# Expert stage of a two-layer encoder: two wide phases, gate and up in chunks of their own, another order of the slots

## What is computed

```python
logits = jnp.dot(xt, router_w, preferred_element_type=jnp.float32)
top_val, top_idx = lax.top_k(logits, TOP_K)
top_w = jax.nn.softmax(top_val, axis=-1)
...
def swiglu(h, w_gate, w_up, w_down):
    return (jax.nn.silu(h @ w_gate) * (h @ w_up)) @ w_down
```

## Time and profile before

| what | us |
|---|---|
| median of 3 runs | 1406.99 (1406.58 to 1407.42) |
| span of the profiled execution | 1403.7 |
| TensorE busy, share of the span | 1304.4, 93% |
| VectorE busy | 415.5 |
| ScalarE busy | 290.6 |
| bytes moved by transfers | 481.98 MB, mean 343 GB/s |

### The profile page before, as it was taken

One profiled execution on the slowest core, in us unless ns is written; L12 is line 12 of the kernel. 1 busy time (PEld: TensorE's weight loads), 2 busy tenths in 40 slices (PEclk: granted clock), 3 DMA queues, 4 the chain that ended last, 5 costly groups with the idle time before them and its releaser, 6 DMA issues.

```text
span 1403.7 us, 24351 instructions
## 1 busy us (share of the span) xinstructions
PE 1304.4 (93%) x10626; PEld 690.9 (49%) x10627; DVE 415.5 (30%) x789; ACT 290.6 (21%) x524; POOL 32.5 (2%) x82
## 2 busy tenths in 40 slices
PE   5999999999999999999999999999589998988986
PEld 5767888888778576243333334333134332324221
DVE  4876844444468664200200000300001200001001
ACT  3346533434333552010000001000001000001000
POOL 1002000000000020000000000000000000000000
PEclk9999999999999999999999999999899999999999
DMA  9988665444575799999989999999999999999996
GB/s 347 332 342 317 198 229 190 180 179 179 223 256 210 325 367 365 400 404 409 407 352 404 365 398 409 408 408 408 409 395 408 409 409 409 409 397 401 408 402 266
DMA packets 146005, 481.98 MB, mean 343 GB/s; under 512 B 9032, under 2 KB 11152, under 8 KB 140784
## 3 DMA queue, kind: packets, MB, share of 16 engines
q1 hardware_dynamic: 141952, 475.06, 87.2%
q10 hardware_dynamic: 2720, 2.93, 0.8%
q0 software_dynamic: 1232, 2.50, 0.6%
HBM read 477.32 MB, written 1.05 MB: 341 GB/s over the span
## 4 chain that ended last, share of the span: by engine, by line
PE 61%; SPq 23%; DMA 7%; DVE 4%; ACT 2%; issue 2%; POOL 0%; DVEq 0%; ACTq 0%
PE ps L2472 19%; SPq L765 15%; PE ps L2524 9%; PE ps L2160 8%; PE ps L2162 8%; PE ps L2161 8%; SPq L779 7%; DMA raw<-in_moe_w_down_dram 4%; PE ps L2082 2%; PE ps L2539 1%; DMA weights<-in_ada_w_dram 1%; DVE weights_lo L1257 1%; PE ps L2241 1%; DMA weights<-in_w_in_dram 1%; PE ps L2214 1%
## 5 line engine op out<-in xcount | busy, mean ns | idle before, releaser
L2472 PE MATMUL ps<-raw,hX 128*32 128x512 f32 (+1 forms) x4416 | 474.2, 583 | 36.0 <-DMA raw<-in_moe_w_up_dram 19.0
L2472 PEld LDWEIGHTS ps<-raw,hX 128*32 128x32 f32 x4416 | 141.2, 110 | 338.9 <-issue 302.7
L2524 PE MATMUL ps<-raw,m_actT 128*32 128x512 f32 x1568 | 180.8, 611 | 18.3 <-DMA raw<-in_moe_w_down_dram 18.2
L2160 PE MATMUL ps<-weights_hi,hT_hi 128*128 128x512 f32 (+1 forms) x416 | 162.1, 390 | 2.7 <-DVE hT_lo L1360 1.5
L2162 PE MATMUL ps<-weights_hi,hT_lo 128*128 128x512 f32 (+1 forms) x416 | 158.9, 382 | 0.0
L2161 PE MATMUL ps<-weights_lo,hT_hi 128*128 128x512 f32 (+1 forms) x416 | 158.7, 381 | 0.0
L1648 DVE TENSOR_TENSOR m_actX<-m_sgX,ps 128x256 f32<-128x256 f32 (+1 forms) x20 | 7.8, 388 | 406.5 <-ACT m_sg L1108 279.9
L2524 PEld LDWEIGHTS ps<-raw,m_actT 128*32 128x32 f32 x1568 | 54.5, 112 | 136.3 <-issue 125.9
L1257 DVE TENSOR_TENSOR weights_lo<-weights,weights_hi 128x2048 fp32r<-128x2048 f32 (+1 forms) x52 | 113.1, 2202 | 2.4 <-ACT weights_hi L934 1.1
L934 ACT ACTIVATE weights_hi<-weights 128x2048 fp32r<-128x2048 f32 (+1 forms) x48 | 87.2, 1839 | 55.6 <-PE ps L2162 51.4
L1651 DVE TENSOR_TENSOR m_act<-m_sg,ps 128x512 f32<-128x512 f32 (+2 forms) x20 | 16.1, 805 | 265.9 <-ACT m_sg L1108 265.9
(11 more groups left out here) (277 smaller groups left out, 1051.0 us busy)
## 6 DMA issues: line engine op xcount, KB each, us to landing
raw<-in_moe_w_gate_dram SPq DMA_DIRECT2D x112, 1024.0 KB, 16.8
raw<-in_moe_w_up_dram SPq DMA_DIRECT2D x112, 1024.0 KB, 18.4
raw<-in_moe_w_down_dram SPq DMA_DIRECT2D x110, 1024.0 KB, 16.8
weights<-in_ada_w_dram SPq DMA_DIRECT2D x18, 2048.0 KB, 9.9
weights<-in_ffn_w_gate_dram SPq DMA_DIRECT2D x14, 1024.0 KB, 5.6
weights<-in_ffn_w_up_dram SPq DMA_DIRECT2D x14, 1024.0 KB, 8.2
weights<-in_ffn_w_down_dram SPq DMA_DIRECT2D x7, 2048.0 KB, 9.6
weights<-in_w_in_dram SPq DMA_DIRECT2D x6, 2048.0 KB, 12.7
```

The costliest lines, as they stand in the source:

```text
L2160: pe.matmul(dst, stat_hi, hi, start=start, stop=False, skip_group_check=True)
L2472: mm = pe.matmul(ps[32 * q:32 * q + 32, bank, 0:2 * w].rearrange("p (g n) -> p g n", g=2), hX[:, k, at32:at32 + 32], weights[:, kk, :, at: ...
L2524: mm = pe.matmul(ps[32 * quarter:32 * quarter + 32, bank, col:col + w], stationary[:, 32 * half:32 * half + 32], raw[buffer][:, D * j + w ...
```

## The change

- Two phases of 2048 and 1536 columns in place of four. A unit is now a whole bank of 512 columns (`COL`, 384 in the second phase) of gate alone; ACT writes its silu to SBUF, then the same bank takes the up sums, and DVE multiplies. TensorE counts up `part` after each unit, so that ACT and DVE go unit by unit; `turned` and `copied` count units too.
- A gate chunk or an up chunk has two k rows of 2048 or 1536 columns: loads of 128 x 2048 (8 KB a row) or 128 x 1536 (6 KB a row). In the second phase a chunk is 1.5 MiB.
- Down chunks take the hidden rows in pairs: partition p holds rows 2p and 2p + 1 of 256, which lie side by side in memory (8 KB); in the second phase a pair and a single row (4 KB). The transposes read the product's columns with a step of two to match.
- Order of a step on TensorE: four gate chunks, two down chunks of the step before, four up chunks, two more down chunks, transposes.
- Slots are now A, X, ABX, X, AX, AB, X, A, in groups (0), (1), (2, 3), (4), (5, 6), (7); banks for gathers and added rows follow.
- The tail is the last two down chunks, in two and three loads.
- Tiles move: some share places with tiles that are no longer needed then. On DVE, `shares`, `token_rows` and `row_numbers` come one phase earlier.

```diff
-NPH = 4
-WIDE = (1024, 1024, 1024, 512)
+NPH = 2
+WIDE = (2048, 1536)
+COL = (512, 384)
 HU = 256
-GU_CHUNKS = (4, 4, 4, 2)
-DOWN_CHUNKS = (2, 2, 2, 1)
+KINDS = ("gate", "up", "down")
+CHUNKS = 4
+
+
+DOWN_RUNS = (((0, 2), (2, 2)), ((0, 2), (2, 1)))
+J = [sum(r for _, r in runs) for runs in DOWN_RUNS]
 RAWS = 9
 EARLY = 2
...
 
-SLOT_RANK = (0, 1, 6, 3, 7, 2, 5, 4)
-SLOT_PASSES = ("A", "ABX", "X", "AX", "X", "AB", "X", "A")
-GROUPS = ((0,), (1, 2), (3, 4), (5, 6), (7,))
+SLOT_RANK = (0, 5, 1, 6, 3, 2, 7, 4)
+SLOT_PASSES = ("A", "X", "ABX", "X", "AX", "AB", "X", "A")
+GROUPS = ((0,), (1,), (2, 3), (4,), (5, 6), (7,))
 OVER_PASSES = "AB"
...
 
+def units_of(passes):
+
+
+    return [(c, b) for c in passes for b in range(len(UNIT_BANKS[c]))]
+
+
+def turn_order(passes):
+
+    return sorted(units_of(passes), key=lambda unit: unit[0] != "X")
+
+
 def chunk_order():
 
     order = []
     for s, n in STEPS:
-        order += [("gu", s, n, i) for i in range(GU_CHUNKS[n])]
-        for t, m in ended_by(s, n):
-            order += [("down", t, m, i) for i in range(DOWN_CHUNKS[m])]
+        for kind, down in (("gate", (0, 1)), ("up", (2, 3))):
+            order += [(kind, s, n, i) for i in range(CHUNKS)]
+            order += [("down", t, m, i) for t, m in step_before(s, n) for i in down]
+        if n == NPH - 1 and s >= LAST - 1:
+            order += [("down", s, n, i) for i in range(CHUNKS)]
     return order
 
...
             def load_chunk(z, sig, e, kind, n, i):
                 b = z.buffer(kind, n, i)
-                if kind == "gu":
-                    per = CH // (2 * WIDE[n])
+                if kind != "down":
                     dst = gu_view(raw[b], n)
-                    for g, view in enumerate((moe_gate_v, moe_up_v)):
-                        src = view[bass.ds(e, 1), :, per * i:per * i + per, 1024 * n:1024 * n + WIDE[n]]
-                        sp.dma_start(dst[:, :, g, :], src.rearrange("a p k n -> p (a k) n")).then_inc(
+                    view = moe_gate_v if kind == "gate" else moe_up_v
+                    for kk in range(2):
+                        k = 2 * i + kk
+                        src = view[bass.ds(e, 1), :, k:k + 1, 2048 * n:2048 * n + WIDE[n]]
+                        sp.dma_start(dst[:, kk:kk + 1, :], src.rearrange("a p k n -> p (a k) n")).then_inc(
                             sig.loaded[b], 16)
-                elif sig is main and (kind, z.s, n, i) in TAIL:
+                    return
+                first = 2048 * n + COL[n] * i
+                in_tail = sig is main and (kind, z.s, n, i) in TAIL
+                if in_tail:
                     at = TAIL.index((kind, z.s, n, i))
...
+                    pieces = [(j, w, tail_loaded[TAIL_FIRST[at] + h]) for h, (j, w) in enumerate(TAIL_RUNS[at])]
                 else:
...
+                    pieces = [(j, w, sig.loaded[b]) for j, w in DOWN_RUNS[n]]
+                for j, w, landed in pieces:
+                    at, r = next((at, r) for at, r in DOWN_RUNS[n] if at <= j < at + r)
+                    rows = moe_down_v[bass.ds(e, 1), first + P * at:first + P * (at + r), :]
+                    src = rows.rearrange("a (p r) n -> p (a r) n", r=r)[:, j - at:j - at + w, :]
+                    dst = raw[b][:, D * j:D * (j + w)].rearrange("p (r n) -> p r n", n=D)
+                    sp.dma_start(dst, src).then_inc(landed, 16)
...
             def silu(sig, z, n):
 
...
+                units = units_of(z.passes)
+                for i, (c, b) in enumerate(units):
+                    if i < len(units) - 1:
+                        act.wait_ge(sig.part, z.part("gate", n, i))
+                    else:
+                        act.wait_ge(sig.used, z.used("gate", n, CHUNKS - 1))
+                    act.activation(unit_act(c, b, n), unit_bank(c, b, n), ACT.Silu).then_inc(sig.silu, 1)
 
             def turned_units(sig, z, n):
...
+                for i, (c, b) in enumerate(turn_order(z.passes)):
+                    act.wait_ge(sig.turned, z.at(n, i))
+                    act.activation(unit_turned(z, c, b, n), unit_bank(c, b, n).rearrange("p (j n) -> p j n", n=P),
+                                   ACT.Copy).then_inc(sig.copied, 1)
...
             def gated(sig, z, n):
...
+
+                units = units_of(z.passes)
+                for i, (c, b) in enumerate(units):
+                    if i < len(units) - 1:
+                        dve.wait_ge(sig.part, z.part("up", n, i))
+                    else:
+                        dve.wait_ge(sig.used, z.used("up", n, CHUNKS - 1))
+                    dve.tensor_tensor(unit_act(c, b, n), unit_act(c, b, n), unit_bank(c, b, n),
+                                      ALU.mult).then_inc(sig.act, 1)
...
+            def unit_sums(sig, z, kind, n, between=lambda i: None):
+
+
+                units = units_of(z.passes)
+                for i in range(CHUNKS):
+                    buffer = z.buffer(kind, n, i)
+                    pe.wait_ge(sig.loaded[buffer], z.loaded(kind, n, i))
+                    if sig is main and (z.s, n) == (0, 0) and kind == "gate":
                         pe.wait_ge(first_rows, i + 1)
                     weights = gu_view(raw[buffer], n)
-                    waited = i > 0 or (n == 0 and (sig is over or z.s == 0))
-                    for c, b in parts:
+                    for u, (c, b) in enumerate(units):
                         bank, r = UNIT_BANKS[c][b], z.rows_at + pass_row(z.passes, c)
-                        if not waited and bank in TURN_AT.values():
-                            pe.wait_ge(sig.copied, z.at(n) - 1)
-                            waited = True
+                        if i == 0 and kind == "up":
+                            pe.wait_ge(sig.silu, z.at(n, u))
+                        elif i == 0:
+                            prior = z.bank_copied(n, bank)
+                            if not isinstance(prior, int) or prior > 0:
+                                pe.wait_ge(sig.copied, prior)
                         rows = PASS_ROWS[c]
                         groups, parts32 = P // rows, rows // 32
-                        w = WIDE[n] // 4 if c == "X" else HU
-                        for kk in range(per):
-                            k = per * i + kk
+                        for kk in range(2):
+                            k = 2 * i + kk
                             for q in range(4):
                                 g, at32 = q // parts32, r + 32 * (q % parts32)
...
+                                at = COL[n] * (groups * b + g)
+                                mm = pe.matmul(ps[32 * q:32 * q + 32, bank, 0:COL[n]], hX[:, k, at32:at32 + 32],
+                                               weights[:, kk, at:at + COL[n]], start=(k == 0), stop=(k == KD - 1),
+                                               skip_group_check=True)
+                        if i == CHUNKS - 1 and u < len(units) - 1:
+                            mm.then_inc(sig.part, 1)
                     mm.then_inc(sig.used, 1)
...
+                    between(i)
...
             def turn_units(sig, z, n):
...
+                units = units_of(z.passes)
+                for c, b in turn_order(z.passes):
+                    pe.wait_ge(sig.act, z.at(n, units.index((c, b))))
+                    bank = UNIT_BANKS[c][b]
+                    for j, r in DOWN_RUNS[n]:
+                        src = unit_act(c, b, n)[:, P * j:P * (j + r)].rearrange("p (m r) -> p r m", r=r)
+                        for at in range(r):
+                            mm = pe.transpose(ps[:, bank, P * (j + at):P * (j + at) + P], src[:, at, :], ident[:])
+                    mm.then_inc(sig.turned, 1)
+
+            def down_sums(sig, z, n, chunks=range(CHUNKS)):
+                if 0 in chunks:
+                    pe.wait_ge(sig.copied, z.at(n, len(units_of(z.passes)) - 1))
+                    if n == 0 and z.down_free:
+                        pe.wait_ge(main.y, z.down_free)
+                    if n == NPH - 1 and not z.starts:
+                        pe.wait_ge(main.y, z.s)
+                for i in chunks:
...
+                unit_sums(main, z, "gate", n, between)
                 if (s, n) == (LAST, NPH - 1):
-                    down_sums(main, z, n - 1, (0,))
+                    down_sums(main, z, n - 1, (0, 1))
+                    unit_sums(main, z, "up", n)
+                    down_sums(main, z, n - 1, (2,))
                     turn_units(main, z, n)
-                    down_sums(main, z, n - 1, (1,))
+                    down_sums(main, z, n - 1, (3,))
                     down_sums(main, z, n)
                     return
                 for t, m in step_before(s, n):
-                    down_sums(main, MainSlot(t), m)
+                    down_sums(main, MainSlot(t), m, (0, 1))
+                unit_sums(main, z, "up", n)
+                for t, m in step_before(s, n):
+                    down_sums(main, MainSlot(t), m, (2, 3))
                 turn_units(main, z, n)
```

## The result

The changed kernel takes **1394.44 us** (median of 4 runs, 1392.25 to 1396.34) against 1406.79 for the kernel before beside it: a ratio of 0.9912, with a 95% interval of 0.9900 to 0.9924. That is 12.35 us faster. Forecast were 1385 us in a range of 1368 to 1399, so direction and range held. The forecast was 9.4 us too optimistic, and the narrower range that it gave for its main case, 1377 to 1393, was missed by 1.4 us.

The account below looks back on a forecast made before the run. The expert stage was taken to be bound by its weight stream, bytes at their rate plus holds for full buffers. Terms -29.0 - 8.8 + 16 = -21.8 us gave 1385 us, range 1368 to 1399.

Parts of the forecast that it names:

- term 1: Expert weight stream: longer rows move faster, 104.4 us a slot in place of 108.2; -29.0 us after the first nine loads' 1.6.
- term 2: Slots 1 and 2 of the old order: two rests of the stream, 5.4 + 3.4 us, go; -8.8 us.
- term 3: About 1070 to 1130 us: TensorE falls 56 us behind, eight other buffers hold 40; +16 us of hold.
- What bounds the kernel: Expert stage, 560 to 1393 us: lasts its bytes at their rate plus holds with all nine buffers full; ends with a transfer.
- The first nine loads don't profit: Loads from 484.5 to 540.5 us go out on the same events as before, so 1.6 us of gain is given back.
- The sign for term 1: Windows in slots 0 and 1 were to show 419 to 424 GB/s.
- What costs nothing: SP's 48 more issues (at most 18 us), ACT and DVE work by unit, and strided transposes were taken to add nothing.
- (a): Rival for the weight stream: long rows give nothing, all run at 409 GB/s; -9 us, 1398 us; chance 0.13.
- (c): Rival for the weight stream: long rows run slower, at 389 GB/s; 1439 us; chance 0.06.
- (d): Rival on the coming hold: no hold, as the buffers carry TensorE's lag after all; 1369 us; chance 0.08.
- (b): Rival: TensorE becomes the bound; half-speed strided transposes make 1399 us, at +22 us nothing is gained; chance 0.11.
- The last down transfer: End of the expert stage: the last load of down rows was to land near 1371 us, before the change 1393.1.

## Why the prediction was right, and where its size was off

| step | forecast, us | shown, us |
|---|---|---|
| term 1, rate by length of row | -29.0 | -24.8 |
| term 2, holds that go | -8.8 | -8.8 |
| term 3, hold that comes | +16 | +16.0 |
| start of the stream | not in the sum | +5.3 |
| sum | -21.8 | -12.3 |

What is shown is read from the two profiled executions, whose stages differ by 12.0 us; the medians differ by 12.35. That the sum agrees to some tenths is luck: 1 GB/s of the free rate is 2 us over the eight slots.

- **What bounds the kernel** was read rightly: the stage ends with a transfer, and bytes over rate plus holds makes its time.
- **Term 1** had the right mechanism, and its size was off by 4.2 us. At 418.4 and 405.6 GB/s, the means over the two long windows of each kernel, a slot of 44.04 MB takes 105.3 and 108.6 us, where the forecast had 104.4 and 108.2; eight slots make -26.4 and with the forecast's own 1.6 us for the first nine loads -24.8. The mis-sized figure is "2.473" us per MiB for 8 KB rows. It came from 424 GB/s over a window of 18 us, on other weights; 56 us of nothing but 8 KB rows of the experts show 420, or 2.497, which is 5.3 us over eight slots. The old slot, reckoned 0.4 us too short, gives 3 of them back. The interpolated 419 GB/s for 6 KB measured 418.
- **The step that failed** is "The first nine loads don't profit ... the same events as before". It counted when these loads go out and how fast their bytes move, and not what comes behind them: after TensorE begins, the stream has to wait for buffers up to 600 us. The profiles show 5.3 us, of which 1.3 stand beside a lowered clock that another execution of the same program part doesn't have; a lighter slot 0 gave back 5.1. The sign for term 1, 419 to 424 GB/s in slots 0 and 1, held in slot 1 only (416 to 421 from 640 to 720 us).
- **Term 2** held: no dip at 725 or 790. Its sign did not: I said TensorE would wait some 60 us in slot 1. The waits view from 600 to 740 us holds 15.6 + 13.2 + 0.9 us on transfers:

```profile
PE ps L2526 <- DMA raw<-in_moe_w_up_dram: 15.6, 8, 3.1
PE ps L2574 <- DMA raw<-in_moe_w_down_dram: 13.2, 6, 3.5
```

  The granted clock in the stretches with such waits is 0.78 to 0.91, between the levels of 2.4 and 1.2 GHz, so the sums themselves took part of the spare time. The text had named this, and the figure of 60 left it out.
- **Term 3** had the mechanism, the size, 16.0 us, and two thirds of the place: 10.8 us lie from 1080 to 1140 us as said, 5.2 already from 880 to 920, in the second phase of slot 2, where ABX of slot 2 with X of slot 3 has outrun the buffers. The working looked only at the end of slot 5's first phase. That the size agrees so closely is luck, as its parts were off. From slot 2's first sums to those that end slot 5's first phase TensorE takes 409 us:

```profile
722.06 36.53 PE L2526 MATMUL ps<-raw,hX 128*32 128x512 f32 x320 [0.68 <-ACT m_actTX L1176]
...
1103.70 27.65 PE L2526 MATMUL ps<-raw,hX 128*32 128x512 f32 x256
```

  The 424 of the forecast hold 8 us for slot 4's last two down chunks, which come after that point; so 416 stand against 409. The stream needs 3 us more at the measured rate. And two of the eight chunks in the other buffers there are of 1.5 MiB, so these hold 15 MiB, 38 us, not 40. By these three figures, an estimate, the hold would have been some 8 us, not 16; the rest isn't traced.
- **What costs nothing** held for SP's issues and the small operations. The strided transposes cost 2.4 us in sum, some 1.4 of it within term 3 by their share there (79 of 133).
- **Rivals.** (a) and (c) are out: the expert rows run at 389 to 420 GB/s, by their length. Here the Trainium skill's rule of 512 B per transfer for the line rate ("DMA: Bandwidth & Descriptors", "Specifications") differs from the runs, which rise up to 8 KB; the measurement decides. (d) is out by the two holds. (b) isn't the changed kernel, but it stands next to it: two orders that moved or shortened the holds ended with TensorE last and gained nothing.
- **The last down transfer** landed at 1384.0 us, not near 1371: the stage got 12.0 us shorter and not 21.8, and it began 2.9 us later.

## What to carry to other kernels

Where a stream and an engine are within a few per cent of each other, a gain on one isn't a price that can be added: the same long rows were worth 22 us with a light TensorE and 7.6 us here, and the old order's holds grew from 8.8 to 20.7 us with the change's rows and chunks. So the holds are worked out anew with the new rate, for the first stretch too and for every point where the lag could exceed the buffers, not only the last. A rate for a sum is read over a stretch long enough, of the same tensors, since 1% of the rate of 8 KB rows was 5 us.

## What the runs showed of the hardware

A load's rows raise the rate up to the longest tried here: 389, 402, 407, 418 and 420 GB/s for 2, 3, 4, 6 and 8 KB, on a queue that is never empty. The same bytes in 225 loads in place of 385 didn't change it (419). Transposes of 128 x 128 in fp32 that read every second column took 290 and 322 ns in place of 277 and 289 (means of 98 and 35). And one core alone drew 420 GB/s over 56 us. The Trainium skill ("DMA: Bandwidth & Descriptors", "Specifications") gives about 358 GB/s as a core's limit at the memory, half of a stack's 716; alone the core isn't held to that half. The 435 GB/s that the same table gives for the fabric wasn't exceeded.
